# One gate input of an encoder layer in seven block products, and router scores computed with the router's columns stationary

## The reference

```
proj = h @ w_in                       # split into xa, ya, uv, zc, xbc, dtc, gates
y_a  = rglru(xa) * gelu(ya)  @ w_a_proj      # branch A: conv, gated linear recurrence
y_b  = sgu(uv)               @ w_b_proj      # branch B
y_c  = ssd(zc, xbc, dtc)     @ w_c_proj      # branch C: 16 heads, chunked scan with decay weights
x = x + (sum of sigmoid(gates) * y) @ w_out
x = x + cross_attention(rmsnorm(x), rmsnorm(mem))
x = x + moe(rmsnorm(x))               # logits = xt @ [w_router_group | w_router_expert] + bias
out = rmsnorm(x)
```

## Time and profile before

| | |
|---|---|
| median of 3 runs | 961.66 us |
| profiled execution | 962.97 us, its span 961.1 us |
| PE busy | 826.0 us (86%) |
| PEld busy | 650.2 us (68%) |
| DVE busy | 340.9 us (35%) |
| ACT busy | 191.8 us (20%) |
| POOL busy | 324.7 us (34%) |
| memory read | 283.08 MB |

### The profile page before, as it was taken

One profiled execution on the slowest core, in us unless ns is written; L12 is line 12 of the kernel. 1 busy time (PEld: TensorE's weight loads), 2 busy tenths in 40 slices (PEclk: granted clock), 3 DMA queues, 4 the chain that ended last, 5 costly groups with the idle time before them and its releaser, 6 DMA issues.

```text
span 961.1 us, 18480 instructions
## 1 busy us (share of the span) xinstructions
PE 826.0 (86%) x8065; PEld 650.2 (68%) x8065; DVE 340.9 (35%) x873; ACT 191.8 (20%) x357; POOL 324.7 (34%) x169
## 2 busy tenths in 40 slices
PE   9999999999999999999999996676676675585675
PEld 8999988889999999999887653333333332343332
DVE  3788323746264434244213451121121221221212
ACT  2342138731231000102012111111110111101102
POOL 5876630038998879996300000000000000000000
PEclk9999999999999999999999998888887988988988
DMA  9854534443564344556698999999999999999994
GB/s 313 254 176 177 177 131 157 151 141 123 176 218 159 133 159 166 176 176 228 223 430 336 401 429 432 430 428 436 426 432 434 425 436 428 428 436 430 424 430 195
DMA packets 58927, 284.95 MB, mean 296 GB/s; under 512 B 6308, under 2 KB 11256, under 8 KB 49912
## 3 DMA queue, kind: packets, MB, share of 16 engines
q1 hardware_dynamic: 54600, 280.84, 73.1%
q10 hardware_dynamic: 4272, 3.32, 1.2%
HBM read 283.08 MB, written 1.06 MB: 296 GB/s over the span
## 4 chain that ended last, share of the span: by engine, by line
PE 63%; DMA 31%; ACT 2%; DVE 2%; POOL 1%; issue 1%; SPq 0%; DVEq 0%; ACTq 0%; POOLq 0%
PE bank L1762 32%; DMA blk<-in_w_gate_up_dram 27%; PE bank L2037 9%; PE bank L1648 7%; PE bank L1757 5%; DMA ring<-in_w_down_dram 3%; PE bank L2002 2%; PE bank L1721 1%; PE bank L2066 1%; PE bank L2050 1%; PE bank L1918 1%; PE bank L1898 1%; DMA ring<-in_w_in_dram 1%; PE bank L1836 0%; PE bank L1857 0%
## 5 line engine op out<-in xcount | busy, mean ns | idle before, releaser
L1762 PE MATMUL bank<-blk,ring 128*128 128x128 f32 x1840 | 213.6, 275 | 0.4 <-POOL blk L592 0.4
L1762 PEld LDWEIGHTS bank<-blk,ring 128*128 128x128 f32 x1840 | 209.4, 192 | 2.0 <-issue 1.9
L2037 PE MATMUL bank<-blk,cbm 128*32 128x256 f32 x1024 | 77.9, 456 | 57.9 <-DMA blk<-in_w_gate_up_dram 57.9
L2037 PE MATMUL bank<-ring,cbm 128*32 128x256 f32 x992 | 75.7, 456 | 55.8 <-DMA ring<-in_w_gate_up_dram 55.8
L1488 DVE TENSOR_TENSOR cbm<-bank,gq 128x256 f32<-128x256 f32 x31 | 13.1, 424 | 264.4 <-PE bank L2002 264.4
L2037 PEld LDWEIGHTS bank<-blk,cbm 128*32 128x32 f32 x1024 | 35.0, 127 | 91.7 <-DMA blk<-in_w_gate_up_dram 64.1
L2037 PEld LDWEIGHTS bank<-ring,cbm 128*32 128x32 f32 x992 | 34.5, 127 | 88.3 <-DMA ring<-in_w_gate_up_dram 57.1
L1648 PE MATMUL bank<-blk,ring 128*128 128x256 f32 x384 | 85.4, 381 | 0.8 <-DVE blk L1410 0.8
L556 POOL TENSOR_TENSOR ring<-ring 128x1024 f32<-128x1024 f32 x20 | 47.4, 2371 | 97.0 <-DVE dec L1208 75.6
L1648 PEld LDWEIGHTS bank<-blk,ring 128*128 128x128 f32 x384 | 72.2, 190 | 11.6 <-DVE blk L1410 1.2
L1762 PE MATMUL bank<-ring 128*128 128x128 f32 x608 | 71.0, 275 | 0.0
(11 more groups left out here) (351 smaller groups left out, 1033.7 us busy)
## 6 DMA issues: line engine op xcount, KB each, us to landing
ring<-in_w_gate_up_dram SPq DMA_DIRECT2D x13, 4096.0 KB, 22.4
blk<-in_w_gate_up_dram SPq DMA_DIRECT2D x12, 4096.0 KB, 22.4
ring<-in_w_in_dram SPq DMA_DIRECT2D x19, 2048.0 KB, 7.8
ring<-in_w_down_dram SPq DMA_DIRECT2D x17, 2048.0 KB, 23.2
blk<-in_w_down_dram SPq DMA_DIRECT2D x13, 2048.0 KB, 24.1
blk<-in_w_gate_up_dram SPq DMA_DIRECT2D x8, 2048.0 KB, 20.0
ring<-in_w_gate_up_dram SPq DMA_DIRECT2D x5, 2048.0 KB, 13.4
ring<-in_w_kv_dram SPq DMA_DIRECT2D x4, 2048.0 KB, 8.0
```

What stands on the lines that cost most here:

```text
L1762: last = mm(out_[:, f], wt[:, k, f * P:(f + 1) * P], xt[:, k, :], start=k == 0, stop=k == 3)
L2037: last = mm(gu_bank(p)[c * WIN:(c + 1) * WIN, 0:2 * SEG], xe[:, xin, 4 * j + k, :], w[:, k, :, c, :], start=4 * j + k == 0, stop=4 * j + k ...
```

## The change

ya is computed like the other slabs: two `strassen` calls, with the heads y3 to y6 put inside them, behind the third and the sixth of the seven products. The weight sums of ya go into `params` (whose gate weights are used up by then) and a part of another block; gA's first two sums go into `params` too. VectorE's folds of ya are split and put into its loop over the heads; GELU is done in place by half. GpSimd's first sum of gA now waits for ya's products like any other, and not for weights(6). In the router the weights become stationary and the tokens move: even blocks of x give the scores in rows 0 to 35 of one bank, odd ones in rows 64 to 99, after a product with zeros that clears the bank. ScalarE copies the bank to SBUF, and a product with a matrix of two shifted identities (made once by VectorE) adds the two halves and turns them back to tokens on the partitions.

```diff
-    order += ["wst0", "u0", "u1", "y0", "u2", "y1", "u3", "y2", "ya0", "y3", "ya1", "y4", "ya2", "y5",
-              "ya3", "y6"]
+    order += ["wst0", "u0", "u1", "y0", "u2", "y1", "u3", "y2"]
+    order += ["y3", "y4"] + seven("ya", 0) + ["y5", "y6"] + seven("ya", 1)
...
         def weight_sums(j):
-            two, one = (5, 8) if j < GATE else (10, 2) if j == GATE else (11, 14)
+            two = block(5) if j < BRANCH else params if j <= GATE else block(11)
+            one = block(8 if j < BRANCH else 10 if j < GATE else 2 if j == GATE else 14)
...
             sp.wait_ge(read["sg"], SGU_G)
+            sp.wait_ge(sem["unit_done"], U[last_of("gA", 0)] + 1)
             part(0, 0, TURNS[0])
...
-                if j == GATE:
-                    pool.wait_ge(sem["w_ready"], KD - 1)
-                if j not in (0, GATE, EARLY):
+                if j == BRANCH:
+                    pool.wait_ge(sem["unit_done"], U[f"lg{KD - 1}"] + 1)
+                if j not in (0, BRANCH, EARLY):
                     pool.wait_ge(sem["product"], 6 * (j - 1) + 2)
...
-                if j not in (0, GATE, EARLY):
+                if j not in (0, BRANCH, EARLY):
                     pool.wait_ge(sem["product"], 6 * (j - 1) + 4)
...
+                if j == BRANCH:
+                    pool.wait_ge(sem["w_ready"], 3)
+                if j not in (0, BRANCH, GATE, EARLY):
                     pool.wait_ge(sem["product"], 6 * (j - 1) + 6)
...
-                            ("v", 1)):
+                            ("v", 1), ("ya", 0), ("ya", 1)):
...
-            for i in range(4):
-                evac(f"ya{i}", yaT, ACT.Gelu_apprx_tanh)
-                if i < 3:
-                    exps(5 + i)
+            def gelu_ya(h):
+                folded("ya", h)
+                m = yaT[:, 4 * h:4 * h + 4, :]
+                a.activation(m, m, ACT.Gelu_apprx_tanh).then_inc(sem["ya_ready"], 1)
+            mids("ya", 0)
+            exps(5)
+            exps(6)
+            gelu_ya(0)
+            mids("ya", 1)
+            exps(7)
+            gelu_ya(1)
...
+            ps = take("rt0")
+            a.copy(logT, ps[:, 0:T]).then_inc(read["rt"], 1)
             ps = take("sq0")
...
             for i in range(2, KD):
                 weights(i)
+                if i in (4, 6):
+                    fold_first("ya", i // 2 - 2, columns(yaT, i // 2 - 2))
                 scan(1)
                 skip(i)
                 if i + 2 < KD:
                     exponents(i + 2)
+                if i in (4, 6):
+                    fold_rest("ya", i // 2 - 2, columns(yaT, i // 2 - 2))
...
+            v.tensor_tensor(added, ident[:, 0:NG + NE], ident[:, WR:WR + NG + NE], ALU.add).then_inc(sem["added_ready"], 1)
             for h in range(XA_HEADS + 1):
...
                 product(2, w21, t_[:, 1]).then_inc(sem["product"], 1)
+                if third is not None:
+                    heads(third)
...
                 product(5, S4, x22).then_inc(sem["product"], 1)
+                if sixth is not None:
+                    heads(sixth)
...
-            for i in range(3):
-                dense(f"ya{i}", hT)
-                heads(3 + i)
-            dense("ya3", hT)
-            heads(6)
+            for h in range(2):
+                begin(f"y{2 * h + 3}")
+                begin(f"y{2 * h + 4}")
+                strassen("ya", h, hT, TA, 0, third=2 * h + 3, sixth=2 * h + 4)
...
-                for t in range(NT):
-                    for k in (2 * i, 2 * i + 1):
-                        mm(bank(f"rt{t}")[:, 0:NG + NE], xT[:, k, t * P:(t + 1) * P], wr[:, k, :],
-                           start=k == 0, stop=k == KD - 1)
+                for k in (2 * i, 2 * i + 1):
+                    row = k % 2 * WR
+                    last = mm(bank("rt0")[row:row + NG + NE, 0:T], wr[:, k, :], xT[:, k, :], start=k < 2, stop=k >= KD - 2)
+                return last
             pe.wait_ge(sem["wr_ready"], 1)
+            mm(bank("rt0")[:, 0:T].rearrange("p (a n) -> p a n", n=P), zeros[0:1, :],
+               zeros[0:1, :].rearrange("p (a n) -> p a n", a=1).to_broadcast([1, NT, P]), start=True, stop=True)
...
+            ps = begin("rt1")
+            pe.wait_ge(sem["added_ready"], 1)
+            pe.wait_ge(read["rt"], 1)
+            for t in range(NT):
+                last = mm(ps[:, t * WR:t * WR + NG + NE], logT[:, t * P:(t + 1) * P], added, start=True, stop=True)
+            end(last)
             for i in range(4):
                 ps = begin(f"tr{i}")
```

More of the change, by code:

```diff
@@ L98, in encoder_kernel @@
     order += ["pt0", "pt1", "o0", "pt2", "o1", "pt3", "o2", "o3"]
-    order += [f"ao{i}" for i in range(4)] + ["sq0", "rt0", "rt1"] + [f"tr{i}" for i in range(4)] + ["rk0", "ct0"]
+    order += [f"ao{i}" for i in range(4)] + ["rt0", "sq0", "rt1"] + [f"tr{i}" for i in range(4)] + ["rk0", "ct0"]
     U = {name: i for i, name in enumerate(order)}
@@ L216, in encoder_kernel @@
         TA, TB = (block(b).rearrange("p (q k t) -> p q k t", q=4, t=P) for b in (6, 9))
-        GATE, EARLY = SEVEN["gA", 0], SEVEN["pA", 0]
+        GATE, EARLY, BRANCH = SEVEN["gA", 0], SEVEN["pA", 0], SEVEN["ya", 0]
         def weight_sums(j):
-            two, one = (5, 8) if j < GATE else (10, 2) if j == GATE else (11, 14)
-            halves_ = [block(two)[:, 0:1024], block(two)[:, 1024:2048], block(one)[:, 0:1024]]
+            two = block(5) if j < BRANCH else params if j <= GATE else block(11)
+            one = block(8 if j < BRANCH else 10 if j < GATE else 2 if j == GATE else 14)
+            halves_ = [two[:, 0:1024], two[:, 1024:2048], one[:, 0:1024]]
             return [m.rearrange("p (k n) -> p k n", k=4) for m in halves_]
         def middles(j):
-            home = block(8 if j < GATE else 2 if j == GATE else 14)
+            home = block(8 if j < BRANCH else 10 if j < GATE else 2 if j == GATE else 14)
             return [home[:, 1024 + i * T:1024 + (i + 1) * T].rearrange("p (f t) -> p f t", f=2) for i in range(4)]
@@ L267, in encoder_kernel @@
         bnst = bnst.rearrange("p (t h) n -> p t h n", t=NT)
+        WR = 64
+        assert NG + NE <= WR
+        logT = prow[:, :, :].rearrange("p a n -> p (a n)")
+        added = first[:, 2 * P:2 * P + NG + NE]
         csT = prow[:, :, :].rearrange("p a n -> p (a n)")
@@ L347, in encoder_kernel @@
             conv_init silu_ready lam_ln alog_exp dt_ready dt_act dta_ready d_ready c_ready
-            ln_var ln_rms vn_ready z_ready v_ready pair_ready a2_ready a_ready a2_min mult_ready yA_ready
+            ln_var ln_rms vn_ready z_ready ya_ready v_ready pair_ready a2_ready a_ready a2_min mult_ready yA_ready
             cs_stored cs_taken exp_ready w_ready yz_ready csq_ready csum_ready
@@ L351, in encoder_kernel @@
             product mid_copied weights_ready combos_ready gate_ready c_rms x1_rms
-            wr_ready early_filled x2sq_ready x2fold x2sum_ready x2_rinv gexp_in gexp_done texp_in texp_done assign_ready
+            wr_ready added_ready early_filled x2sq_ready x2fold x2sum_ready x2_rinv gexp_in gexp_done texp_in texp_done assign_ready
              ov_ready half_done gu_done gathered dn_done xn3_ready xe_ready chosen_ready hot_ready placed_ready
@@ L1087, in fold, with fold_first, fold_rest @@
             def fold(name, h, quarter):
+                fold_first(name, h, quarter)
+                fold_rest(name, h, quarter)
+            def fold_first(name, h, quarter):
+                sums(SEVEN[name, h], quarter(1, 1)).then_inc(read["s"], 1)
+            def fold_rest(name, h, quarter):
                 j = SEVEN[name, h]
@@ L1091, in fold @@
                 b2, b3 = bank(f"s{4 * j + 2}"), bank(f"s{4 * j + 3}")
-                sums(j, quarter(1, 1)).then_inc(read["s"], 1)
                 dve.wait_ge(sem["product"], 6 * j + 6)
@@ L1283, in _ @@
                                       ALU.mult, ALU.add))
-            dve.wait_ge(read["ya"], 4)
+            dve.wait_ge(sem["ya_ready"], 2)
             v.tensor_tensor(xaT, xaT, yaT, ALU.mult).then_inc(sem["yA_ready"], 1)
@@ L1422, in _ @@
             lf = rt2("l")
+            ps = take("rt1")
             for t in range(NT):
-                ps = take(f"rt{t}")
-                v.scalar_tensor_tensor(out=lf[:, t, :], in0=ps[:, 0:NG + NE], scalar=stat[:, 20 + t:21 + t],
-                                       in1=br[:, :], op0=ALU.mult, op1=ALU.add).then_inc(read["rt"], 1)
+                last = v.scalar_tensor_tensor(out=lf[:, t, :], in0=ps[:, t * WR:t * WR + NG + NE],
+                                              scalar=stat[:, 20 + t:21 + t], in1=br[:, :], op0=ALU.mult, op1=ALU.add)
+            last.then_inc(read["rt"], 1)
             dve.wait_ge(read["rt"], NT)
@@ L1739, in steps, with strassen @@
                 end(last)
-            def strassen(name, h, x, t_, made, in_rows=False):
+            def strassen(name, h, x, t_, made, in_rows=False, third=None, sixth=None):
                 j = SEVEN[name, h]
@@ L1831, in heads @@
```

(22 more changed lines are left out.)

## The result

The changed kernel takes 965.45 us (median of 6 runs, 963.61 to 966.35) where the kernel before takes 961.33 beside it: a ratio of 1.004, 95% interval 1.003 to 1.005. It is slower by 4.1 us; forecast was 1.7 slower, in a range from 957.5 to 966.0. The profiled execution took 963.93.

What follows compares the result with a forecast made beforehand. TensorE was taken to bound the kernel to about 517 us, then the experts' DMA stream it releases. The ya stage's +1.9 and the router's -0.2 gave +1.7 on 961.66, so 963.4 us, range 957.5 to 966.0.

Steps and rivals of the forecast that it cites:

- GpSimd holds VectorE: ya stage: VectorE's SBUF instructions wait out each running GpSimd sum, making TensorE stand 3.8 at y4 and 1.45 at y6.
- one exponent between D and S2, the rest behind S2, weights(4) held by S4: Ahead of y4: GpSimd's second, third and fourth sums delay VectorE's exponents and decay weights; TensorE stands for 3.8 us.
- forecast 3.8 and 1.45: ya stage: predicted TensorE stalls in us, 3.8 ahead of heads y4 and 1.45 ahead of heads y6.
- The rival in which VectorE keeps its turn: ya stage: GpSimd's sums hold nobody up, so no stall and 958.1 us; chance 0.26.
- the one in which only y4 stalls: ya stage: y6's exponents pass in a gap between GpSimd's sums, 1.45 less, 962.0 us; chance 0.06.
- that in which one more turn is lost: ya stage: VectorE waits out another sum of 2.2, y3 or y5 also late, up to 965.6 us; chance 0.18.
- -3.38 if nothing waits: ya stage on TensorE: products in seven replace four dense units, 31.64 becomes 28.26 us without stalls.
- -3.38 + 3.8 + 1.45 = +1.9: ya stage: saving on products plus stalls at y4 and y6, a net loss of 1.9 us.
- The router, -0.2: Router ahead of the experts' stream: cheaper scores less the added clearing product, -0.2 us, from -0.7 to +0.5.
- forecast 0.59: Router: two score products of 256 columns on array halves take 0.59 us instead of 0.81.
- forecast 0.25: Router: the clearing product adds 0.25 us to the path ahead of ao0, between 0 and 0.4.
- forecast 0.2: Router: the issue behind ao3 moves by 0.2 us less than the ya stage moved it.

Runs made afterwards that it cites:

- e3: Changed kernel plus four waits that start GpSimd's sums only when VectorE has finished decay weights; 959.03 us, ratio 0.9976 to the kernel before.
- e6: Changed kernel with heads y4 and y6 behind the seventh product instead of the sixth, GpSimd's waits unchanged; 966.24 us, ratio 1.005 to the kernel before.
- e4: Changed kernel with 14 idle products on TensorE in front of heads y4; 962.88 us, ratio 1.0012 to the kernel before.
- e5: Changed kernel with waits only on the second ya half's GpSimd sums, none on gA's; 964.99 us, ratio 1.0036 to the kernel before.
- e8: The changed kernel measured again, nothing edited; 964.93 us, ratio 1.0038 to the kernel before.
- e1: Changed kernel with the old router, so only the ya edits; 964.65 us, ratio 1.0034 to the kernel before.
- e2: Kernel before with only the new router, ya still dense; 961.40 us, ratio 1.000 to the kernel before.
- e7: Changed kernel with y4 and y6 behind the seventh product, four waits pacing GpSimd's sums, and earlier router clearing; 959.82 us, ratio 0.9984 to the kernel before.

## Why the prediction was right, and where it was not

**GpSimd holds VectorE: right, shown by e3.** The instructions stalled where the prediction put them: one exponent between D and S2, the rest behind S2, weights(4) held by S4, heads waiting at y4 and y6 only. y4 was forecast at 195.88 for a stage from 180.55, that is at 15.33 of the stage; it came at 15.23. The timeline gives the stalls:

```profile
195.24 0.90 PE L1872 MATMUL bank<-dec,ring 128*64 128x256 f32 x4 [3.32 <-DVE dec L1234]
...
212.47 0.66 PE L1872 MATMUL bank<-dec,ring 128*64 128x256 f32 x4 [1.05 <-DVE dec L1234]
```

They are 3.32 and 1.05, forecast 3.8 and 1.45. Taking GpSimd's turns out of the way (e3) removed both. The rival in which VectorE keeps its turn needed sg near 208.8 and fell at the first row (it began at 215.33); the one in which only y4 stalls fell with y6's 1.05; that in which one more turn is lost did not come in the changed kernel, but e6 shows such a loss (y5, 5.51). The Trainium skill (SBUF — State Buffer, "Who interferes with whom") has the shared ports held for a whole instruction. The sets of 3.41 beside one sum and of 5.51 beside two agree.

**"-3.38 if nothing waits": mis-sized.** e3 measured -2.42 (29.22 - 31.64). The step took the products' price from slabs without heads between the parts, and the restart of 0.19 behind each pair was not counted: five of them are the 0.96 that is missing. A part of the stalls' difference to their forecast is this too: longer parts ask for the heads later, so each stall is shorter by what the parts in front of it grew.

**The sum as a whole: a term was missing.** By the prediction the stage was -3.38 + 3.8 + 1.45 = +1.9. By the rows it is -2.42 + 3.32 + 1.05 + 1.6 = +3.55, and 0.14 more for the heads that wait (0.88 instead of 0.81, twice): +3.69, against 3.68 measured. Without the clock's 1.6 the errors in the other terms nearly cancel (+2.09 against +1.9), which is luck. So is it that 965.45 lies inside the range: its upper part was there for one more lost turn of VectorE (up to 965.6), and what filled it was the clock. The fall was not forecast, although what it came behind, an empty TensorE in the middle of dense products, was; and e4 shows that it goes when TensorE is not empty. The Trainium skill (TensorE: Matmul & The Clock Gate, "HAM oscillation — how this bites in real kernels") warns that products behind a gap without work start at the lower clock. The rows of e5 and e6 agree; in the changed kernel and in e8 the heads still begin at 1.00 and the fall to 0.50 comes 0.3 and 0.8 us behind their start; and e1's profiled execution, with the same gap of 3.32 at y4, has no fall. What decides it in one execution was not tried.

**The router, -0.2: nothing that shows.** The scores came at 0.56 (forecast 0.59), the clearing at 0.28 (forecast 0.25), the issue behind ao3 0.08 less late than gA (forecast 0.2). What the scores saved came back in part in the units behind them. In the chain of before, ao2 and ao3 read

```profile
502.56 6.99 PE bank L1648 x32
...
510.37 6.99 PE bank L1648 x32
```

and they take 7.10 and 7.12 now. With ao0 and ao1 0.07 shorter (14.01 against 14.08) that is 0.28 - 2 x 0.25 + 0.11 + 0.13 - 0.07 = -0.05. e2 (ratio 1.000) agrees.

**What is left.** Stage, sg and router make 3.68 - 0.20 - 0.05 = +3.4. The medians differ by 4.1; in e8 by 3.7 (964.93 against 961.26). e4, without the fall, has no such rest: its stage gives 33.74 - 31.64 - 0.20 - 0.05 = +1.85, and its median is 1.5 above that of before (962.88 against 961.41). So the rest seems to go with the fall, which would then cost more in other executions than the 1.6 of this one. No trace shows that: the changed kernel's runs lie up to 3.3 apart, and a profile shows one of them.

## What to carry to other kernels

Before work is given to GpSimd, lay its turns beside VectorE's chain for the next consumer: here each sum in between cost a whole turn, and a sum that was put off collided with the next one that was due. So pace all of the turns by VectorE's progress, or none (e3 against e5), and look whether TensorE then waits for a sum that is held back (e7). A stall of TensorE of some 3 us in dense work can cost more than its length: here a few us of products at half speed came on top, in some executions and not in all. A price read off an uninterrupted stretch holds only there; count the changes between forms of products too.

## What the runs showed of the hardware

- The clock fell to 0.50 with stalls of 3.32 (after), 3.31 (e8), 3.43 (e6) and 4.78 (e5), and stayed there for 3 to 6 us of the work behind them. In e1 it stayed at 1.00 behind a stall of 3.32, and it did not fall behind those of 1.05 and 1.64.
- Products that do no work, in front of waiting heads, kept the clock at 1.00 in the profiled execution and brought about 2 us of the median back (e4).
- Between back-to-back sums of GpSimd, VectorE got about one instruction in at each boundary: 2.37 for an exponent of some 0.3, 3.41 to 3.50 for a set of decay weights of 1.40 beside one sum, 5.51 beside two.
- A stretch of full-array products behind a pair of half-array heads costs 0.19 to 0.20 more than the same products behind their own kind; moving the pairs moved that cost (e7, where sg paid it), and did not save it.
